# Gate and up projections by seven block products for eight in 20 of 22 tile pairs, with t kept in HBM

## The reference

```python
h = rms_norm(x, norm_ffn[l]) * (1.0 + scale2) + shift2
ffn = (jax.nn.silu(h @ w_gate[l]) * (h @ w_up[l])) @ w_down[l]
x = x + gate2 * ffn
```

## Time and profile before

| what | us |
|---|---|
| median of three runs | 1500.77 |
| the profiled execution | 1499.38 |
| its span, first to last instruction | 1497.6 |
| TensorE busy in it | 1393.3 |
| VectorE busy | 658.2 |
| ScalarE busy | 476.2 |
| GpSimd busy | 86.3 |

### The profile page before, as it was taken

One profiled execution on the slowest core, in us unless ns is written; L12 is line 12 of the kernel. 1 busy time (PEld: TensorE's weight loads), 2 busy tenths in 40 slices (PEclk: granted clock), 3 DMA queues, 4 the chain that ended last, 5 costly groups with the idle time before them and its releaser, 6 DMA issues.

```text
span 1497.6 us, 18059 instructions
## 1 busy us (share of the span) xinstructions
PE 1393.3 (93%) x6960; PEld 1165.0 (78%) x6960; DVE 658.2 (44%) x921; ACT 476.2 (32%) x727; POOL 86.3 (6%) x84
## 2 busy tenths in 40 slices
...
GB/s 382 25 216 98 168 126 88 1 1 1 1 1 43 1 1 1 141 1 29 56 140 57 42 56 42 56 42 42 56 42 56 42 56 127 97 90 175 128 98 98
DMA packets 24995, 109.56 MB, mean 73 GB/s; under 512 B 2800, under 2 KB 2928, under 8 KB 23408
## 3 DMA queue, kind: packets, MB, share of 16 engines
...
...
## 4 chain that ended last, share of the span: by engine, by line
PE 77%; DVE 14%; issue 4%; POOL 2%; ACT 2%; DVEq 0%; DMA 0%; SPq 0%; POOLq 0%; ACTq 0%
PE ps L1288 45%; PE ps L1277 8%; PE ps L1279 8%; PE ps L1278 8%; DVE left L1083 4%; PE ps L1484 2%; PE ps L1506 1%; DVE acc L846 1%; PE ps L1493 1%; DVE beta L1087 1%; PE ps L1473 1%; POOL rstd L408 1%; PE ps L1564 1%; DVE sqs L831 1%; POOL rstd L410 1%
## 5 line engine op out<-in xcount | busy, mean ns | idle before, releaser
L825 DVE TENSOR_TENSOR WL<-raw,WH 128x1024 fp32r<-128x1024 f32 x114 | 141.1, 1238 | 457.3 <-ACT WH L462 457.3
L462 ACT ACTIVATE WH<-raw 128x1024 fp32r<-128x1024 f32 x114 | 120.3, 1056 | 357.7 <-PE ps L1288 185.1
L1288 PE MATMUL ps<-h2H,WH 128*128 128x512 f32 x672 | 207.0, 389 | 0.0
L1288 PE MATMUL ps<-h2L,WH 128*128 128x512 f32 x672 | 206.9, 389 | 0.0
L1288 PE MATMUL ps<-h2H,WL 128*128 128x512 f32 x672 | 206.8, 389 | 0.0
L1288 PEld LDWEIGHTS ps<-h2H,WH 128*128 128x128 f32 x672 | 126.0, 188 | 26.4 <-DVE WL L825 0.2
L1288 PEld LDWEIGHTS ps<-h2L,WH 128*128 128x128 f32 x672 | 126.1, 188 | 26.2
L1288 PEld LDWEIGHTS ps<-h2H,WL 128*128 128x128 f32 x672 | 126.1, 188 | 26.2
L1277 PE MATMUL ps<-TH,WH 128*128 128x512 f32 x352 | 137.1, 389 | 1.0 <-DVE yst L1249 1.0
L1278 PE MATMUL ps<-TL,WH 128*128 128x512 f32 x352 | 137.0, 389 | 0.0
L1279 PE MATMUL ps<-TH,WL 128*128 128x512 f32 x352 | 136.9, 389 | 0.0
...
## 6 DMA issues: line engine op xcount, KB each, us to landing
...
```

Source lines behind the costliest of these rows:

```text
L462: A(WH[par % 2][:], raw[r % 2][:], ACT.Copy).then_inc(sem["split_h"], 1)
L825: V.tensor_tensor(WL[par % 2][:], raw[r % 2][:], WH[par % 2][:], ALU.subtract).then_inc(sem["split_l"], 1)
L1288: last = mm(ps[:, b + hf, :], l[s][:, j * P:(j + 1) * P], r[:, j, 512 * hf:512 * hf + 512], start=(j == 0 and k == 0), stop=(j == KD - 1 a ...
```

## The change

The matrix of weights of a pair is cut into four blocks: gate and up, each in the lower and the upper half of the 1024 input features (G1, G2, U1, U2). The data is cut the same way, feature half by token half (X11, X12 are the lower features, X21, X22 the upper). Eight block products give the pair in both token halves. The identity in Winograd's form takes seven: with S1 = U1 + U2, S2 = S1 - G1, S3 = G1 - U1, S4 = G2 - S2 and T1 = X12 - X11, T2 = X22 - T1, T3 = X22 - X12, T4 = X21 - T2, TensorE forms in this order S2 T2, S1 T1, G1 X11, S3 T3, G2 X21, U2 T4, S4 X22. `product` is one of them: 4 feature blocks x 3 matmuls of 512 columns into one bank. G2 X21 is added onto the bank of G1 X11 once ScalarE has copied that (`s1`), S4 X22 onto that of S1 T1 once VectorE has read it (`c22`). VectorE's five additions u2, u3, c22, c21, c12 give up and gate of the second half and up of the first; two silu and two products give t.

Pairs 0 and 1 stay as they were. While pair 1 runs, the sums of the data are made (`tA`, `tB`, `t1`, `t2`, `t4` with high and low parts); T3 is written over X12, so X12's place in `h2H` and `h2L` changes after tile 3 (the up tile of pair 1). For this the modulated input is kept in fp32 as well, `h2f`: VectorE scales into it, and ScalarE adds the shift in place (`shift_half`). For each of the 20 other pairs SP loads gate and up weights together (1 MB, `sraw`), VectorE makes four weight sums, ScalarE and VectorE split seven operands (`slH`, `slL`) one pair ahead. t no longer has room in SBUF: each pair's t goes to HBM (`t_d`), and each down tile reads its half of it back (`traw`) beside its weights (`draw`). The GpSimd read of `xres` waits for the last product in place of the last tile. Loops are written out. The diff, cut to its core:

```diff
...
+NQ = 7
+Q_S2, Q_S1, Q_G1, Q_S3, Q_G2, Q_U2, Q_S4 = range(NQ)
+B_U2, B_E, B_A, B_C, B_D = range(5)
+Q_BANK = [B_U2, B_E, B_A, B_C, B_A, B_D, B_E]
...
+    gs = [at("gs0", [P, S], F32, 78), at("gs1", [P, S], F32, 82)]
...
+    sraw = [at("sraw0", [P, 2, 2, 512], F32, 126), at("sraw1", [P, 2, 2, 512], F32, 82)]
+    ssum = at("ssum", [P, 4, 512], F32, 118)
...
+        def load_pair(u):
+            f = N_STD + u
+            if u >= 2:
+                sp.wait_ge(sem["g_l"], NQ * (u - 2) + Q_U2 + 1)
+            sp.dma_start(sraw[u % 2][:].rearrange("p g k n -> p g (k n)"), gu_d[2 * f:2 * f + 2].rearrange("g p n -> p g n")).then_inc(sraw_in[u % 2], 16)
+        def store_t(f):
...
+                sp.wait_ge(sem["g_t"], 2 * (f - N_STD) + 2)
+                sp.dma_start(t_d[f], tst[f % 2][:]).then_inc(t_out[f % 2], 16)
...
+        load_pair(0)
+        store_t(0)
+        store_t(1)
+        sp.wait_ge(sem["x_l"], 3)
+        sp.wait_ge(t_out[1], 16)
+        load_pair(1)
+        for u in range(NSU):
+            if u + 2 < NSU:
+                load_pair(u + 2)
+            if u < NSU - 1:
+                store_t(N_STD + u)
+        def load_down(d):
+            hf, f = d // NF, d % NF
+            if d < 2:
+                sp.wait_ge(sem["g_mm"], NQ * (NSU - 1) + (Q_S2 if d == 0 else Q_S1) + 1)
+            else:
+                sp.wait_ge(sem["d_l"], d - 1)
+            sp.dma_start(draw[d % 2][:], down_d[f]).then_inc(d_in[d % 2], 16)
+            if d < 2:
+                sp.wait_ge(sem["g_mm"], NQ * (NSU - 1) + Q_G1 + 1)
+                sp.wait_ge(t_out[d % 2], 16)
+            else:
+                sp.wait_ge(sem["tl_done"], d - 1)
+            sp.dma_start(traw[d % 2][:], t_d[f, :, 512 * hf:512 * hf + 512]).then_inc(traw_in[d % 2], 16)
...
+        store_t(NF - 1)
+        sp.wait_ge(t_out[0], 16 * (NF // 2))
+        sp.wait_ge(t_out[1], 16 * (NF // 2))
+        for d in range(2, 2 * NF):
+            load_down(d)
...
+        def shift_half(n):
+            hf, j = n // KD, n % KD
+            x = h2f[:, j, 512 * hf:512 * hf + 512]
+            act.wait_ge(sem["h2L_done"], n + 1)
+            A(x, x, ACT.Identity, bias=mod2[:, 8 + j:9 + j]).then_inc(sem["h2f_done"], 1)
         for n in range(2 * KD):
...
             hf, j = n // KD, n % KD
             act.wait_ge(sem["xn2_done"], n + 1)
-            A(h2H[:, j, 512 * hf:512 * hf + 512], xn2[j % 2][:], ACT.Identity, bias=mod2[:, 8 + j:9 + j]).then_inc(sem["h2H_done"], 1)
...
+            A(h2H[:, j, 512 * hf:512 * hf + 512], h2f[:, j, 512 * hf:512 * hf + 512], ACT.Identity, bias=mod2[:, 8 + j:9 + j]).then_inc(sem["h2H_done"], 1)
+            if n >= 2:
+                shift_half(n - 2)
+        split(H_GU + 2, H_GU + 2, 0)
+        shift_half(2 * KD - 2)
+        shift_half(2 * KD - 1)
+        def sum_high(k, dst, src):
+            act.wait_ge(sem["x_s"], k + 1)
+            A(dst, src[:], ACT.Copy).then_inc(sem["x_h"], 1)
+        act.wait_ge(sem["x2_spill"], 16)
+        sum_high(0, t1H[:], tA)
+        sum_high(1, t2H[:], tB)
+        act.wait_ge(sem["pe_tile"], after(H_GU))
+        A(gs[0][:], pair(0), ACT.Silu).then_inc(sem["silu_done"], 1)
+        split(H_GU + 3, H_GU + 3, 0)
+        sum_high(2, t4H[:], tA)
+        def slot_high(u, q):
+            if q in (Q_G1, Q_G2, Q_U2):
+                act.wait_ge(sraw_in[u % 2], 16 * (u // 2 + 1))
...
+                act.wait_ge(sem["g_s"], 4 * u + (Q_S1, Q_S3, Q_S2, Q_S4).index(q) + 1)
+            A(slH[q][:], operand(u, q), ACT.Copy).then_inc(sem["g_h"], 1)
...
+        for q in range(NQ):
+            slot_high(0, q)
+        act.wait_ge(sem["x_l"], 3)
+        act.wait_ge(sem["pe_tile"], after(H_GU + 2))
+        A(gs[1][:], pair(4), ACT.Silu).then_inc(sem["silu_done"], 1)
+        act.wait_ge(sem["pe_tile"], after(H_GU + 3))
+        A(h2H[:, 0:4, 512:S], tB[:], ACT.Copy).then_inc(sem["x_h"], 1)
+        for u in range(NSU):
+            for q in range(NQ):
+                act.wait_ge(sem["g_mm"], NQ * u + q + 1)
+                if q == Q_G1:
+                    if u:
+                        act.wait_ge(sem["g_c"], 5 * (u - 1) + 1)
+                    A(s1[:], ps[:, B_A, :], ACT.Copy).then_inc(sem["g_s1"], 1)
+                if q == Q_G2:
+                    if u:
+                        act.wait_ge(sem["g_t"], 2 * (u - 1) + 1)
+                    A(sg1[:], ps[:, B_A, :], ACT.Silu).then_inc(sem["g_silu"], 1)
+                if u + 1 < NSU:
+                    slot_high(u + 1, q)
...
+            act.wait_ge(sem["g_c"], 5 * u + 5)
+            A(sg2[:], c12[:], ACT.Silu).then_inc(sem["g_silu"], 1)
...
+        def down_split(d):
+            if d < 2:
+                act.wait_ge(sem["g_mm"], NQ * NSU)
+            else:
+                act.wait_ge(sem["d_tile"], d - 1)
+            act.wait_ge(traw_in[d % 2], 16 * (d // 2 + 1))
+            A(TH[d % 2][:], traw[d % 2][:], ACT.Copy).then_inc(sem["th_done"], 1)
+            act.wait_ge(d_in[d % 2], 16 * (d // 2 + 1))
+            A(dWH[d % 2][:], draw[d % 2][:], ACT.Copy).then_inc(sem["d_h"], 1)
...
-                if n >= 2:
-                    dve.wait_ge(sem["h2L_done"], n - 1)
-                V.scalar_tensor_tensor(xn2[j % 2][:], x2[:, j, 512 * hf:512 * hf + 512], a2[:, j:j + 1], ps[:, 6 + hf, :], ALU.mult, ALU.mult).then_inc(sem["xn2_done"], 1)
+                V.scalar_tensor_tensor(h2f[:, j, 512 * hf:512 * hf + 512], x2[:, j, 512 * hf:512 * hf + 512], a2[:, j:j + 1], ps[:, 6 + hf, :], ALU.mult, ALU.mult).then_inc(sem["xn2_done"], 1)
...
+        dve.wait_ge(sem["h2f_done"], 2 * KD)
+        V.tensor_tensor(tA[:], block_of(0, 1), block_of(0, 0), ALU.subtract).then_inc(sem["x_s"], 1)
+        dve.wait_ge(sem["x_s"], 1)
+        V.tensor_tensor(tB[:], block_of(1, 1), tA[:], ALU.subtract).then_inc(sem["x_s"], 1)
+        dve.wait_ge(sem["x_h"], 1)
+        V.tensor_tensor(t1L[:], tA[:], t1H[:], ALU.subtract).then_inc(sem["x_l"], 1)
+        std_gate(0)
+        dve.wait_ge(sem["x_s"], 2)
+        dve.wait_ge(sem["x_l"], 1)
+        V.tensor_tensor(tA[:], block_of(1, 0), tB[:], ALU.subtract).then_inc(sem["x_s"], 1)
+        wsplit(H_GU + 3, H_GU + 3)
+        dve.wait_ge(sem["x_h"], 2)
+        V.tensor_tensor(t2L[:], tB[:], t2H[:], ALU.subtract).then_inc(sem["x_l"], 1)
+        dve.wait_ge(sem["x_l"], 2)
+        V.tensor_tensor(tB[:], block_of(1, 1), block_of(0, 1), ALU.subtract).then_inc(sem["x_s"], 1)
+        dve.wait_ge(sem["x_h"], 3)
+        dve.wait_ge(t_out[0], 16)
+        V.tensor_tensor(t4L[:], tA[:], t4H[:], ALU.subtract).then_inc(sem["x_l"], 1)
+        def weight_sums(u):
+            w = sraw[u % 2]
+            dve.wait_ge(sraw_in[u % 2], 16 * (u // 2 + 1))
+            V.tensor_tensor(ssum[:, 0, :], w[:, 1, 0, :], w[:, 1, 1, :], ALU.add).then_inc(sem["g_s"], 1)
+            V.tensor_tensor(ssum[:, 2, :], w[:, 0, 0, :], w[:, 1, 0, :], ALU.subtract).then_inc(sem["g_s"], 1)
+            dve.wait_ge(sem["g_s"], 4 * u + 1)
...
+        def slot_low(u, q):
+            if u < NSU:
+                dve.wait_ge(sem["g_h"], NQ * u + q + 1)
+                V.tensor_tensor(slL[q][:], operand(u, q), slH[q][:], ALU.subtract).then_inc(sem["g_l"], 1)
+        def combine(dst, src, bank):
+            V.tensor_tensor(dst[:], ps[:, bank, :], src[:], ALU.add).then_inc(sem["g_c"], 1)
+        dve.wait_ge(sem["x_s"], 4)
+        weight_sums(0)
+        for q in range(NQ):
+            slot_low(0, q)
+        std_gate(1)
+        dve.wait_ge(sem["x_h"], 4)
+        V.tensor_tensor(h2L[:, 0:4, 512:S], tB[:], h2H[:, 0:4, 512:S], ALU.subtract).then_inc(sem["x_l"], 1)
+        def finish_t(u):
+            dve.wait_ge(sem["g_silu"], 2 * u + 2)
+            V.tensor_tensor(tst[u % 2][:, 512:S], c22[:], sg2[:], ALU.mult).then_inc(sem["g_t"], 1)
+        for u in range(NSU):
+            if u + 1 < NSU:
+                weight_sums(u + 1)
+            if u:
+                finish_t(u - 1)
+            slot_low(u + 1, Q_S2)
+            slot_low(u + 1, Q_S1)
+            dve.wait_ge(sem["g_s1"], u + 1)
+            combine(u2, s1, B_U2)
...
+            V.tensor_tensor(tst[u % 2][:, 0:512], c21[:], sg1[:], ALU.mult).then_inc(sem["g_t"], 1)
+            dve.wait_ge(sem["g_mm"], NQ * u + Q_S4 + 1)
+            combine(c12, u2, B_E)
+            slot_low(u + 1, Q_S4)
+        finish_t(NSU - 1)
...
+        x_block = {Q_S2: (t2H, t2L), Q_S1: (t1H, t1L), Q_U2: (t4H, t4L)}
...
+        def product(u, q):
+            xh, xl = x_block[q]
+            for c in range(4):
+                w = slice(c * P, (c + 1) * P)
+                for k, (l, r) in enumerate(((slH, xh), (slH, xl), (slL, xh))):
+                    last = mm(ps[:, Q_BANK[q], :], l[q][:, w], r[:, c, :], start=(c == 0 and k == 0 and q not in (Q_G2, Q_S4)),
+                              stop=(c == 3 and k == 2), skip_group_check=True)
+            last.then_inc(sem["g_mm"], 1)
+        pe.wait_ge(sem["t_done"], after(0))
+        for u in range(NSU):
...
```

(42 more changed lines are left out.)

228 lines of the change are left out of this document (133 added, 95 removed).

## The result

The changed kernel took 1460.78 us (median of four runs, 1459.45 to 1461.65), the kernel before 1499.80 in the same comparison: ratio 0.9736, 95% interval 0.9724 to 0.9749. Forecast were 1463.8 us and a range of 1452 to 1479. The profiled execution took 1459.45 us, its span 1457.5, 40.1 us less than the span before.

The account below looks back on a forecast made before the run. TensorE's matmul count times pace was taken as the bound. -54.4 - 0.75 + 2.7 + 6.0 + 4.7 + 0.8 + 4.0 = -37.0 from 1499.38, plus 1.4 for the median, gave 1463.8 us; range 1452 to 1479, own 1455 to 1474.

Parts of the forecast that it names:

- The saving: Gate and up stage: 84 matmuls a pair for 96, 2.72 us less in each of 20 pairs, -54.4 us.
- Steady pairs cost nothing: Steady pairs by the identity: VectorE's 11.3 and ScalarE's 6.2 us fit in 19.04 us of TensorE, 0 us of wait.
- rival 2: Each pair's load comes late behind the store of t: 19 more waits and clock falls, +152 us, 1616; chance 0.04.
- Boundaries cost nothing: Ends of products in one bank, with one or two waits before the next: no cost in the forecast.
- Rival 1: Each of 140 product ends in one bank exposes 0.1 us: 14 us in all, 1478; chance 0.08.
- The modulation: Stage before tile 2: full-size h2f removes VectorE's wait for reused staging tiles, -0.75 us, bounds -1.5 and +1.
- Tile 3: Entry to the new stage: tile 3 starts 2.7 us late (1.5 to 4.5), waiting for its low weights.
- The fifth product: G2 in the first identity pair waits for copy s1, behind pair 1's late load: 6.0 us once (4 to 9).
- The entry to down: First down tile waits 4.7 us (3.5 to 6) for its split; third tile's late loads add 0.8 (0 to 3).
- The clock: Falls to half after the 6.0 and 4.7 us waits, none after the 2.7: +4.0 us (0 to 7).
- The prediction's own sign: Part ahead of the change: the prediction is wrong if the span before 760 us moves.

Follow-up runs that it names:

- experiment 7: Changed kernel with the product S1 T1 formed twice in each of the 20 pairs, 12 matmuls more a pair; 1510.80 us, ratio 1.0072 to the kernel before.
- Experiment 8: Changed kernel with each 1 MB load of pairs 2 to 19 issued only after the previous pair's second product; 1558.35 us, ratio 1.039 to the kernel before.
- experiment 5: Changed kernel with only the split of tile 3's weights moved earlier on ScalarE and VectorE; 1460.86 us, ratio 0.974 to the kernel before.
- experiment 1: Changed kernel with s1, u2, u3 and c22 of the first identity pair put ahead of the next pair's operands; 1456.41 us, ratio 0.971 to before.
- Experiments 2 to 4: Changed kernel with first two down tiles' splits in the last pair (1463.91 us), t reads awaiting only their own store (1457.72), or both, third-tile loads earlier (1454.41).

## Why the prediction was right, step by step

**The saving.** 54.4 us by 19.04 us a pair: measured to the digit, and by experiment 7 from the other side. The pace of 0.2267 us carried over to twelve matmuls in a row into one bank.

**Steady pairs cost nothing.** Confirmed, no idle in 355 us. Experiment 8 turned rival 2 into fact with its mechanism, a wait for s1 and a fall of the clock in every pair: the rival did not come true because the load had the slack worked out, and it would have made the kernel slower. Its price was smaller than the rival's, 5.4 us a pair (96.5 over 18) against 8.0. The Trainium skill (TensorE: Matmul & The Clock Gate, section A second HAM failure mode: psum-queue depth-cycling) reports a clock that swings when groups over several banks have small idles between them. The traces agree as far as they go: the clock was at 0.91 where idles of 3.2 us and more were put into each pair; in the changed kernel seven products over five banks ran at 1.00 throughout.

**Boundaries cost nothing.** Rival 1 had 14 us for 140 product ends; the period of 19.04 leaves nothing for them.

**The modulation.** -0.75 forecast, -0.48 measured, with a fall of the clock in it that the forecast did not have. The five traces without that fall have -0.64 to -0.70.

**Tile 3.** 2.7 forecast, 2.40 measured, for the stated reason. What the prediction did not say is that this wait was worth little: experiment 5 shows the chain behind it, and removing it alone gave nothing.

**The fifth product.** Right place, releaser and cause (experiment 1); the size was 6.0 for 3.94. The product was due at 827.17 instead of 828.1 and released at 830.97 instead of 834.1. Pair 1's t was finished 1.4 us earlier than laid out, its store landed in 2.6 us where I took 3.9, and the load in 4.83 instead of 5.2. The formula of the Trainium skill (DMA: Bandwidth & Descriptors, section Anatomy of one DMA), which the page gives for DMAs that GpSimd issues while this load is SP's, had given an estimated 4.4 for the load; the measured 4.83 lies halfway between it and the row.

**The entry to down.** 4.7 forecast, 4.34 of idle and 0.16 of restart measured. The third tile waited 1.39 where 0.8 was in the sum. Experiments 2 to 4 show the two as one row of waits.

**The clock.** 4.0 forecast for two falls, 3.38 measured; it fell after the waits of 3.94 and 4.34 us and not after 2.40 and 1.39. The places are as forecast, the size is in part luck: at the first down tile, behind the same 4.34 us, experiment 1 lost 2.9 us. And the third fall, behind 2.20 us in the modulation, was not forecast.

**Left over.** The waits came out 2.1 us below the sum (1.5 with their restarts), the clock 0.6. Another 1.35 us came ahead of the changed code: in nine traces (this kernel and its variants, with the same program up to there) the spill of x2 was issued between 764.10 and 767.06 us, and at 765.67 before. That scatter of 3 us is the execution's, not the change's. Without it the change is worth 38.7 us, against a sum of 37.0. The prediction's own sign, that it is wrong if the span before 760 us moves, was too strict for a trace of one execution. Its own range is a little narrow too: the bounds of its terms, all taken at once, give 1454 to 1477 and not 1455 to 1474; the stated range holds both.
